# Search stage of a two-layer hybrid decoder: GpSimd takes over two mixer steps, VectorE counts the smallest block, early output units move into the attention heads

## The reference, cut to what matters

```python
p = h @ w_in
sc, q, k, v, iq, ik, iw = jnp.split(p, EVEN_SPLIT, axis=-1)
bg, cg, hv = jnp.split(sc, 3, axis=-1)
ya = bg * causal_dwconv(cg * hv, conv_w)          # mixer A, 512 channels, 3 taps
...
isc = jnp.einsum('bhqs,bqh->bqs', isc, iwb)       # isc was relu(query . key) of the indexer
_, idx = lax.top_k(isc, topk)                     # 256 keys per query, then softmax attention: yb
...
x = x + jnp.concatenate([ya, yb], axis=-1) @ w_out
```

## Time and profile before

| what | value |
|---|---|
| median of 3 runs | 2160.55 us (2159.86 to 2162.41) |
| profiled execution, its own time | 2160.83 us |
| its span | 2159.1 us |
| PE busy | 2061.6 us (95%) |
| DVE busy | 1380.4 us (64%) |
| ACT busy | 1099.8 us (51%) |
| POOL busy | 1098.5 us (51%) |

### The profile page before, as it was taken

The page is one execution under the profiler, slowest core; times in us unless marked ns, Lnnn a source line. Parts: engine busy times, 40 slices in busy tenths (PEclk is TensorE's granted clock), DMA queues, the critical chain, the costliest instruction groups (busy, mean ns, idle before and its releaser), DMA issues. The chain is left out here.

```text
span 2159.1 us, 30031 instructions
## 1 busy us (share of the span) xinstructions
PE 2061.6 (95%) x11390; PEld 1005.8 (47%) x11390; DVE 1380.4 (64%) x1992; ACT 1099.8 (51%) x1655; POOL 1098.5 (51%) x843
## 2 busy tenths in 40 slices
PE   8989977889999999999999999989999999999998
PEld 5544435654444444444444445655444444444444
DVE  7788888858675575575554036685867467467552
ACT  6468947635664564555323224443566466465520
POOL 6014324225667767756584023513486866766642
PEclk9999989999999999999999999999999999999999
DMA  5001100002112212212231011102121221211212
GB/s 180 17 11 49 35 27 2 14 27 61 56 49 69 59 49 68 59 47 64 65 112 52 0 30 35 45 7 64 39 59 44 74 59 44 68 55 49 59 44 93
DMA packets 186493, 110.20 MB, mean 51 GB/s; under 512 B 4351, under 2 KB 180902, under 8 KB 186358
## 3 DMA queue, kind: packets, MB, share of 16 engines
q1 hardware_dynamic: 185894, 107.00, 16.6%
q0 software_dynamic: 464, 1.39, 0.2%
HBM read 104.18 MB, written 4.19 MB: 50 GB/s over the span
## 5 line engine op out<-in xcount | busy, mean ns | idle before, releaser
L1277 PE MATMUL ps<-arena 128*128 128x512 f16 x2712 | 594.0, 379 | 3.9 <-DVE ps L2869 2.5
L1277 PEld LDWEIGHTS ps<-arena 128*128 128x128 f16 x2712 | 264.8, 98 | 326.6 <-DVE ps L2869 5.5
L1277 PE MATMUL ps<-h_hi,arena 128*128 128x512 f16 x1216 | 371.8, 381 | 4.6 <-DVE arena L2960 4.0
L805 POOL TENSOR_SCALAR w_scaled<-stage 128x1024 f32<-128x1024 f32 (+4 forms) x82 | 80.2, 978 | 575.6 <-PE ps L1136 410.3
L2878 DVE SCALAR_TENSOR_TENSOR work<-ps,fvec,work 128x1023 f32<-128x1023 f32 (+1 forms) x176 | 221.7, 1279 | 21.8 <-ACT work L2046 18.7
L1277 PE MATMUL ps<-h_lo,arena 128*128 128x512 f16 x608 | 231.9, 381 | 0.0
L1277 PEld LDWEIGHTS ps<-h_hi,arena 128*128 128x128 f16 x1216 | 119.4, 98 | 151.4 <-issue 7.7
L1136 PE MATMUL ps<-arena 128*128 128x512 f16 x708 | 157.1, 383 | 15.1 <-DVE xT L2747 12.8
L859 POOL TENSOR_TENSOR w_scaled<-stage 128x512 f32<-128x512 f32 (+2 forms) x62 | 70.0, 1129 | 194.4 <-ACT stage L1767 194.2
L1767 ACT ACTIVATE stage<-stage 128x2048 f32<-128x2048 f32 (+2 forms) x62 | 104.6, 1686 | 112.8 <-DMA stage<-in_ffn_w_up_dram 97.1
L1136 PE MATMUL ps<-h_hi,arena 128*128 128x512 f16 x576 | 149.9, 381 | 1.7 <-ACT small L1949 1.7
(11 more groups left out here) (382 smaller groups left out, 3844.5 us busy)
## 6 DMA issues: line engine op xcount, KB each, us to landing
stage<-in_ffn_w_up_dram SPq DMA_DIRECT2D x84, 512.0 KB, 3.8
stage<-in_ffn_w_down_dram SPq DMA_DIRECT2D x48, 384.0 KB, 3.2
stage<-in_od_w_in_dram SPq DMA_DIRECT2D x20, 512.0 KB, 3.8
stage<-in_ev_w_in_dram SPq DMA_DIRECT2D x12, 512.0 KB, 3.8
arena<-in_x_dram SPq DMA_DIRECT2D x8, 512.0 KB, 5.9
stage<-in_ffn_w_down_dram SPq DMA_DIRECT2D x16, 256.0 KB, 2.7
out_dram<-arena SPq DMA_DIRECT2D x8, 512.0 KB, 3.0
stage<-in_od_w_out_dram SPq DMA_DIRECT2D x12, 256.0 KB, 2.7
```

The source lines that it names most:

```text
L805: nc.gpsimd.tensor_scalar(scaled, src, W_SCALE, 1.0, ALU.mult, ALU.mult).then_inc(w_parts, 1)
L1277: last = mm(ps[:, bank, :], left, b[:, k, :], start=(fresh and k == 0 and pss == 0), stop=(k == nk - 1 and pss == 2), skip_group_check=True)
```

## The change

The far tap and the high of mixer A go from ScalarE to GpSimd, whose queue gets them by hand between its splits: tap i behind the `ev_sc` split 3i+3, high i behind split 3i+4 (the last tap and high behind the first and second `ev_out_a` split). The two nearer taps are two separate steps now. Tiles of mixer A are 8 steps apart instead of 7, gates stand at steps 1, 10, 18 and 26. The last second product and the last low stand behind the search. In the 13 steps in which VectorE has no mixer work, VectorE and not ScalarE counts block 2, from a negated copy of its scores. Early units alternate between pairs 0 and 1 for the first four; two can be made before any add. All early adds stand behind the search: units 0 to 3 before the first head, 4 after head 3, 5 to 7 at heads 8, 14 and 20. Scores of blocks 2 and 3 use one bank each; block 4's first scores wait for the last early add. The repeated counts stand mostly before and in front of the first heads.

```diff
-MIX_EVERY, MIX_GATE, MIX_PROD, MIX_TAPS, MIX_SECOND, MIX_LOW = 7, 2, 4, 6, 7, 8
+MIX_EVERY, MIX_PROD, MIX_NEAR_TAP, MIX_FAR_TAP, MIX_SECOND, MIX_LOW = 8, 4, 5, 6, 7, 9
+MIX_GATE_BITS = (1, 10, 18, 26)
+VECTOR_MIX_BITS = [at + MIX_EVERY * i for at in (MIX_PROD, MIX_NEAR_TAP, MIX_FAR_TAP, MIX_SECOND, MIX_LOW) for i in range(4)]
+SHARED = 2
+SHARED_BY_DVE = [bit for bit in range(SEARCH_BITS) if bit not in VECTOR_MIX_BITS]
-EARLY_BIT = 27
 EARLY_ALONE = 4
+EARLY_HEADS = {2: 4, 8: 5, 14: 6, 20: 7}
...
+score_negated = att[:, 1, 512:512 + P * (SHARED + 1)]
...
 def score_banks(b, h):
-    return ps[:, 2 + h % 2, :] if b < 2 else pair(h % 2)
+    return ps[:, 2 + h % 2, :] if b < 4 else pair(h % 2)
+def early_pair(m):
+    return pair(m % 2 if m < EARLY_ALONE else 0)
...
-    split_section("ev_sc", 6, 2, peeled=6)
-    split_section("ev_out_a", 2, 4, words=lambda u: EARLY_KS * P)
+    def mixer_tap(i):
+        pool.wait_ge(a_prod, i + 2)
+        nc.gpsimd.tensor_scalar(work[:, 2, :], work[:, 1, :], vec[:, VEC_AT["sc_conv"] + 8 + i:VEC_AT["sc_conv"] + 9 + i], None,
+                                ALU.mult).then_inc(a_tap, 1)
+    def mixer_high(i):
+        pool.wait_ge(a_f, i + 3)
+        nc.gpsimd.tensor_scalar(mix_hi[:, i, :], work[:, 1, :], 1.0, 1.0, ALU.mult, ALU.mult).then_inc(a_hi, 1)
+    for u in range(12):
+        split_ring(unit0["ev_sc"] + u, u, 1024, ring0["ev_sc"] + u if u >= 2 else None)
+        if u >= 3 and u % 3 == 0:
+            mixer_tap(u // 3 - 1)
+        if u >= 3 and u % 3 == 1:
+            mixer_high(u // 3 - 1)
+    split_ring(unit0["ev_out_a"], 0, EARLY_KS * P, ring0["ev_out_a"])
+    mixer_tap(3)
+    split_ring(unit0["ev_out_a"] + 1, 1, EARLY_KS * P, ring0["ev_out_a"] + 1)
+    mixer_high(3)
+    with pool.Fori(0, 3) as i:
+        for u in range(2):
+            split_ring(unit0["ev_out_a"] + 2 + u + i * 2, u, EARLY_KS * P, ring0["ev_out_a"] + 2 + u + i * 2)
...
         if m == 0:
             pe.wait_ge(a_f, 5)
+        elif m == 1:
+            pe.wait_ge(a_cg, 5)
         else:
-            pe.wait_ge(early_added, EARLY0 + m)
+            pe.wait_ge(early_added, EARLY0 + (m - 1 if m < EARLY_ALONE else m))
-        three_pass(m % 2, EARLY_KS, mix_hi, mix_lo, 0, pair(0), True, True).then_inc(unit_done, 1)
+        three_pass(m % 2, EARLY_KS, mix_hi, mix_lo, 0, early_pair(m), True, True).then_inc(unit_done, 1)
     def scores(n):
-        if n == 2 * HEADS:
+        if n == 4 * HEADS:
             pe.wait_ge(early_added, EARLY0 + KT)
         dst = score_banks(b, h)
...
+    pe.wait_ge(early_added, EARLY0 + EARLY_ALONE)
-        if n % 2 == 0 and n // 2 < KT - EARLY_ALONE:
-            early_unit(EARLY_ALONE + n // 2)
+        if n in EARLY_HEADS:
+            early_unit(EARLY_HEADS[n])
...
-    def mixer_tap(i):
-        act.wait_ge(a_prod, i + 2)
-        A(work[:, 2, :], work[:, 1, :], ACT.Copy,
-          scale=vec[:, VEC_AT["sc_conv"] + 8 + i:VEC_AT["sc_conv"] + 9 + i]).then_inc(a_tap, 1)
-    def mixer_high(i):
-        act.wait_ge(a_f, i + 3)
-        A(mix_hi[:, i, :], work[:, 1, :], ACT.Copy).then_inc(a_hi, 1)
     def sign_count(b):
-    def mixer_part(bit, at, operation):
-        i, r = divmod(bit - at, MIX_EVERY)
-        if r == 0 and 0 <= i < 4:
-            operation(i)
     for bit in range(SEARCH_BITS):
         act.wait_ge(cand_ready, 2 * bit if bit else 1)
         for b in ACT_GROUPS[0]:
-            last = sign_count(b)
+            if b != SHARED or bit not in SHARED_BY_DVE:
+                last = sign_count(b)
         last.then_inc(act_counted, 1)
         act.wait_ge(cand_ready, 2 * bit + 1)
         for b in ACT_GROUPS[1]:
             last = sign_count(b)
         last.then_inc(act_counted, 1)
-        mixer_part(bit, MIX_SECOND, mixer_high)
-        mixer_part(bit, MIX_GATE, mixer_gate)
-        mixer_part(bit, MIX_PROD, mixer_tap)
+        if bit in MIX_GATE_BITS:
+            mixer_gate(MIX_GATE_BITS.index(bit))
...
+    shared = SEARCH.index(SHARED)
+        V.tensor_scalar(score_negated, score[SHARED][:], -1.0, None, ALU.mult)
+        dve.wait_ge(cand_ready, 1)
+        ts_(V.tensor_copy(srch[:, S_V, allc], srch[:, S_BACK, allc]))
+        ts_(V.memset(srch[:, S_V, shared:shared + 1], TOPK - 0.5))
-    def take(cols):
-        return V.tensor_tensor(srch_i[:, S_TAKE, cols], srch[:, S_COUNT, cols], srch[:, S_BACK, cols], ALU.is_ge)
+    def take(cols, back=S_BACK):
+        return V.tensor_tensor(srch_i[:, S_TAKE, cols], srch[:, S_COUNT, cols], srch[:, back, cols], ALU.is_ge)
+    def count_shared():
+        return V.tensor_scalar(flags[shared][0], score_negated, srch[:, S_CAND, shared:shared + 1], None, ALU.is_le,
+                               ALU.add, accum_out=srch[:, S_COUNT, shared:shared + 1])
...
+        by_dve = bit in SHARED_BY_DVE
+        if by_dve:
+            counted_shared = step_(count_shared())
         for c, b in enumerate(BY_DVE):
             last = count(S_CAND, b, c)
         counted = step_(last)
         dve.wait_ge(act_counted, 2 * bit + 1)
-        took = step_(take(early_cols))
+        if by_dve:
+            dve.wait_ge(top_step, counted_shared)
+        took = step_(take(early_cols, S_V if by_dve else S_BACK))
...
-    def mixer_taps(i):
-        tap = VEC_AT["sc_conv"]
-        dve.wait_ge(a_tap, i + 1)
-        for j in (1, 0):
-            s = 2 - j
-            V.scalar_tensor_tensor(out=work[:, 2, s:], in0=work[:, 1, 0:T - s],
-                                   scalar=vec[:, tap + 4 * j + i:tap + 4 * j + i + 1], in1=work[:, 2, s:],
-                                   op0=ALU.mult, op1=ALU.add).then_inc(a_step, 1)
-            if j:
-                dve.wait_ge(a_step, 2 * i + s)
+    def mixer_tap(i, j):
+        tap, s = VEC_AT["sc_conv"], 2 - j
+        if j:
+            dve.wait_ge(a_tap, i + 1)
+        else:
+            dve.wait_ge(a_step, 2 * i + 1)
+        V.scalar_tensor_tensor(out=work[:, 2, s:], in0=work[:, 1, 0:T - s], scalar=vec[:, tap + 4 * j + i:tap + 4 * j + i + 1],
+                               in1=work[:, 2, s:], op0=ALU.mult, op1=ALU.add).then_inc(a_step, 1)
...
     def add_early(m):
         dve.wait_ge(unit_done, ring0["ev_out_a"] + m + 1)
-        V.scalar_tensor_tensor(out=xT[:, m, :], in0=pair(0), scalar=W_UNSCALE, in1=xT[:, m, :],
+        V.scalar_tensor_tensor(out=xT[:, m, :], in0=early_pair(m), scalar=W_UNSCALE, in1=xT[:, m, :],
     def mixer_part(bit):
-        for at, operation in ((MIX_PROD, mixer_prod), (MIX_TAPS, mixer_taps), (MIX_SECOND, mixer_second), (MIX_LOW, mixer_low)):
+        for at, operation in ((MIX_PROD, mixer_prod), (MIX_NEAR_TAP, lambda i: mixer_tap(i, 1)),
+                              (MIX_FAR_TAP, lambda i: mixer_tap(i, 0)), (MIX_SECOND, mixer_second), (MIX_LOW, mixer_low)):
-        if 0 <= bit - EARLY_BIT < EARLY_ALONE:
-            add_early(bit - EARLY_BIT)
...
     search_begin()
     for bit in range(SEARCH_BITS):
         search_bit(bit, lambda: mixer_part(bit))
+    mixer_second(3)
     resolve_limits()
-    attend(0, 2)
-    add_early(4)
+    add_early(0)
     count_part(S_TRY, 0)
-    attend(2, 4)
-    add_early(5)
+    add_early(1)
     count_part(S_TRY, 1)
     resolve_take()
+    add_early(2)
+    add_early(3)
+    attend(0, 2)
+    mixer_low(3)
+    count_part(S_BACK, 0, ALU.is_gt, last=1)
+    attend(2, 4)
+    add_early(4)
+    count_part(S_BACK, 1, ALU.is_gt, last=1)
+    resolve_room()
     attend(4, 6)
+    rank(2)
+    attend(6, 10)
+    add_early(5)
+    attend(10, 16)
     add_early(6)
-    count_part(S_BACK, 0, ALU.is_gt)
-    attend(6, 8)
+    attend(16, 22)
     add_early(7)
-    count_part(S_BACK, 1, ALU.is_gt)
-    resolve_room()
-    rank(2)
-    attend(8, HEADS * NB + 2)
+    attend(22, HEADS * NB + 2)
     V.memset(small[:, 59:60], 0.0).then_inc(x_added, 2)
     output(NB - 1)
     evict(NB - 1, None)
```

More of the change, by code:

```diff
@@ L2684, in resolve_limits, with count_part @@
                 ts_(V.copy_predicated(back, neg, near))
-            def count_part(row, part, op=ALU.is_ge):
+            def count_part(row, part, op=ALU.is_ge, last=0):
                 for c in range(3 * part, 3 * part + 3):
-                    ins = count(row, SEARCH[c], c, op, last=1)
+                    ins = count(row, SEARCH[c], c, op, last)
                 if part:
```

## The result

The changed kernel takes 2173.16 us (median of 6 runs, 2168.88 to 2174.98); the kernel before, run beside it, 2161.82 (2159.86 to 2164.37). The ratio is 1.0046, with a 95% interval of 1.0036 to 1.0056: 11.3 us slower, more than the 0.2% that counts as a difference, and 2 us above the predicted range. The profiled execution took 2174.98 us, its span is 2173.2 against 2159.1 before. Two executions behind the numbers of this document, one of experiment 5 (2709 us) and one of the kernel before (2226 us), ran at a lower mean clock, 0.75 and 0.94, and stand outside the ratios.

A forecast was written before the change was run, and what follows sets the result against it. With TensorE 95% busy, the threshold search, paced by held VectorE operations, was taken to bound its stage. Terms -9.4 + 4.6 + 4.7 = -0.1 us against 2160.83 profiled (median 0.3 lower) gave 2160.5, own range 2156 to 2166, overall 2147 to 2171.

The forecast's parts named there:

- The search, -9.4 us: Threshold search: would end near 283 us instead of 292.27, 9.4 us earlier, with ScalarE relieved but VectorE operations still held.
- The stepping: Search steps played through in the new order: eight steps take 35.2 us, 4.40 each against 4.44 before.
- The two rows that were to show what is **not** held: Search: a 640-column count (0.87 us) and second product (1.21) beside GpSimd subtractions, read as counts and products not held.
- The tap, 1.2 us: Far tap on GpSimd in the search: priced at 1.2 us from the normalisation L778, 1.22 us for 1024 columns.
- Rival two: Search: the tap costs L987's 3.70 us, shifting four taps and their splits 2.5 us each; +10, 2170 us; chance 0.20.
- From the search's end to the ninth head, 29.7 us: Stretch behind the search with early units 0 to 4: 29.7 us against 25.1 before, so 4.6 us more.
- The 13.4 behind it: First to ninth head: low 1.2, six counts 5.4, one early unit with add 1.5, six heads, room and rank 5.3.
- Units 5 to 7 among the heads, 4.7 us: Blocks 1 to 3: three early units mostly covered by scored heads and a rank cost 4.7 us; bounds 3.7 and 16.1.
- Rival three: Heads of blocks 1 to 3: early units there cost their whole present chain, +11 us, 2171; chance 0.09.
- The shared count: Search: block 2's count moved to VectorE in 13 steps, taking 0.60 us of ScalarE's time in each.
- Rival four: Search: shared count does nothing because VectorE is late; pace stays 4.44, search ends at 286, 2164 us; chance 0.09.
- Behind the heads: Rest of the kernel: heads remain VectorE's work as before, a shift of their start goes to the end; 0 change.

The follow-up runs named there:

- experiment 5: Changed kernel with early units 5 to 7 issued at heads 10, 18 and 26 and added behind the ranks of blocks 3 to 5: 2163.97 us, ratio 1.0008.
- kernel 1: Changed kernel with one edit, GpSimd's far tap given a second multiplication by 1.0: 2170.03 us, ratio to the kernel before 1.0037.
- experiment 8: Tap put back to one multiplication in a fast-tap kernel (2157.36 us) whose early additions stand in the search's last steps and block 0 again: 2160.96 us, ratio 1.0000.
- experiment 4: Changed kernel, slow tap kept, but ScalarE counts block 2 in all 31 steps instead of sharing with VectorE: 2172.60 us, ratio 1.0055.

## Why the prediction was wrong

It forecast no change (2160.5), with 0.36 for slower; measured is 11.3 us slower, beyond the upper end of 2171.

**The search, -9.4 us.** Right in kind, too large: -7.3 by the end's place (284.99 against 292.27), -7.5 from the first opener to the end. That held operations set the pace was right, and the places of the steps came out close: step 8 was forecast at 184.3 and opens at 184.70, step 24 at 256.0 and opens at 256.82. That they came out so close is partly luck. The stepping priced the tap at 1.2 us; in kernel 1, where it has that price, step 24 opens at 253.77 and the search ends at 281.3, not near 283, so a tap priced too low was set against steps taken too long. (Two groups of 35.2 us from 184.3 give 254.7, not the 256.0 written down.) The steps before 27 gained nothing, and the whole gain came in steps 27 to 30, from which the early additions and their waits were gone. What the sum set down as a faster search was mostly work moved behind it; with the fast tap the first 27 steps do gain, 116.9 us against 119.5.

The two rows that were to show what is **not** held began 0.15 us before the subtraction beside them, so they could not show it. Other rows do: in the kernel before, the count of 512 columns at 161.97, begun 0.65 us into the same subtraction, took 0.74 us, and in the changed kernel the addition at 297.79, with one operand in PSUM and begun 0.18 us into a subtraction, took its plain 1.23.

**The tap, 1.2 us.** This was the row chosen wrongly: 2.85 us, between L778's 1.22 and L987's 3.70. The nearest row had a second multiplication, and that is just what makes the difference: 1.12 us with it, 2.85 without. It cost 4.05 us in the search and about 3.1 in the time (experiment 1; 3.3 and 3.6 in experiment 8). Rival two had the direction, but its mechanism and size fell: the small operations are held 1.12 us, not the tap's whole length, and the loss is 1.0 us per tap, not 2.5. The Trainium skill's GPSIMD Engine Reference (section 4.1, Engine selection), whose "roughly line-rate" for one-input work would give the 1.2 us, holds for the two-multiplication form and not for this one.

**From the search's end to the ninth head, 29.7 us.** Measured 32.46. The first head came 16.95 us after the end (forecast 16.3), close, but by two misses that cancel. The limits took 3.5 us (286.12 to 289.63) and not 1.4, held by GpSimd's last high and the splits behind it. So the first addition ended late and unit 2, which waits for it, began 5.9 us in and not 4.5; then the pair took 9.32 us and not 10.16. The 13.4 behind it was 15.5: unit 4 ran 5.74 us at a lowered clock and left VectorE waiting 1.80 us, where 1.5 in the open was set down with its addition. The clock in that window (302 to 317 us) was 0.79. In kernels 1 and 4, with the fast tap and with the slow one, unit 4 took 4.05 us and the stretch is 13.82.

**Units 5 to 7 among the heads, 4.7 us.** The step that failed most: 12.6 us, near the far bound of 16.1. I had the two heads already scored cover 1.4 and 3.4 us, rank(4) the third (the first of these, 3.9 less 1.4 and an addition of 1.2, gives 3.7 and not the 3.2 in the sum), and took off 1.5 for catching up and the clock. In the trace heads 8 and 9 were through when unit 5 had hardly begun (VectorE idles from 319.0, the unit runs from 318.08), nothing was caught up, and the unit took 5.50 us and not 3.9. The cover I counted was work of the same chain, and it ends when TensorE begins. Rival three named this cost (+11) and gave it 0.09; its picture, the whole chain exposed, was nearly right for units 5 and 6, and wrong as a rule, since three units under ranks cost 4.6 (experiment 5).

**The shared count.** Rival four, that it does nothing because VectorE is late, is nearly what experiment 4 shows: 1.3 us on the search, none that could be told in the time. I had it pay with ScalarE as the pace setter.

**Behind the heads.** 1.4 us more than nothing (0.9 between heads 32 and 63); no run isolates it, and it is within what the same stretch differs between the other profiles.

## What to carry to other kernels

Before moving a block of TensorE work whose result another engine must add, ask what that engine has queued **independent of it** at that place: the price of the same units went from 1.5 us each, little more than the addition (under ranks), over 2.1 to 2.7 (beside counts) to 4.2 (between heads that wait for TensorE). A stage that ends earlier because work left it has gained nothing until that work is placed where something covers it; sum both sides of the border. And price an instruction by a row of its very form: one operand slot more or less changed GpSimd's multiplication by 2.5 times.

## What the runs showed of the hardware

- GpSimd's multiplication of 128x1024 float32 by a column takes 2.85 us with one operation (second scalar None) and 1.12 us as two multiplications, the second by 1.0; the four of each kernel agree within 0.02 us. I had expected the shorter form to be no slower.
- The slow form holds VectorE's instructions with two operands in SBUF only for its first 1.12 us: in the changed kernel the four takes that began 0.09 to 0.33 us into it all ended 1.12 us after its start, and the next two instructions ran free. Why, no run shows.
- Not only instructions with two operands are held. In the changed kernel's resolving, beside GpSimd's last high and a split, a TENSOR_SCALAR with one tensor operand took 1.04 us (286.32) and a COPY 0.90 us (288.42), each to the end of GpSimd's instruction; in the kernel before the same two take 0.17. Counts with an accumulated sum were not held (0.74 us at 161.97 before).
- The holding works both ways: in the changed kernel GpSimd's subtraction that began just behind VectorE's near tap took 3.10 us instead of 2.13, three times (3.11, 3.10, 3.09).
- TensorE's mean granted clock in the changed kernel's stretches between heads 0 and 16 was 0.71 to 0.82, so parts of each ran at the lower of its two levels (1.2 and 2.4 GHz). A unit of 18 matmuls took 4.05 to 5.77 us among the heads, and unit 4, at one and the same place, 5.74 in the changed kernel and 4.05 in kernels 1 and 4.
